# A SwiGLU down projection in split fp32r, with the FFN width worked in two halves

## The reference, cut to what matters

```python
h = h + mix
xn = rmsnorm(h, norm_ffn)
gate, up = split_cols(xn @ ffn_w_gu, (FFN_HIDDEN, FFN_HIDDEN))     # 1024 x 5632
h = h + (jax.nn.silu(gate) * up) @ ffn_w_down                      # 2816 x 1024
y = rmsnorm(h, norm_final)
```

## Time and profile before

| what | value |
| --- | --- |
| median of 3 runs | 3121.63 us |
| the profiled execution: its span, first to last instruction | 3120.6 us |
| gate and up, first matmul to the first of down | 2283.98 to 2784.48 us of the span |
| down, to the start of the last norm's sums | 2784.48 to 3089.9 us |
| last norm and stores | 3089.9 to 3120.6 us |
| mean granted TensorE clock | 0.933 |

### The profile page before, as it was taken

One profiled execution on the slowest core, in us unless ns is written; L12 is line 12 of the kernel. 1 busy time (PEld: TensorE's weight loads), 2 busy tenths in 40 slices (PEclk: granted clock), 3 DMA queues, 4 the chain that ended last, 5 costly groups with the idle time before them and its releaser, 6 DMA issues.

```text
span 3120.6 us, 46699 instructions
## 1 busy us (share of the span) xinstructions
PE 2861.2 (92%) x19365; PEld 2259.2 (72%) x19365; DVE 975.0 (31%) x1690; ACT 706.4 (23%) x1113; POOL 19.1 (1%) x26
## 2 busy tenths in 40 slices
PE   5979797989999999999999999964979999999997
PEld 3657575757777686868677786853979999986665
DVE  1120302035354453636354443636131111110001
ACT  2221202122232322222232322221132222210000
POOL 0000000000000000000000000000000000000000
PEclk8989797979998999999998999956989999999999
DMA  3010101000000000000000000002001111120111
GB/s 132 14 70 0 69 0 69 28 15 1 29 2 29 2 29 2 19 11 2 29 2 29 2 29 2 28 15 108 27 27 47 47 47 47 45 78 19 37 37 54
DMA packets 19098, 99.84 MB, mean 32 GB/s; under 512 B 4544, under 2 KB 4736, under 8 KB 15120
## 3 DMA queue, kind: packets, MB, share of 16 engines
q1 hardware_dynamic: 17328, 88.44, 7.7%
q0 software_dynamic: 1632, 9.21, 0.8%
HBM read 86.31 MB, written 11.34 MB: 31 GB/s over the span
## 4 chain that ended last, share of the span: by engine, by line
PE 89%; DVE 6%; issue 2%; ACT 2%; DMA 0%; DVEq 0%; SPq 0%; ACTq 0%
PE bank L502 89%; ACT arena L870 1%; DMA arena<-in_consts 0%; DVE arena L1418 0%; DVE arena L1269 0%; DVE arena L1417 0%; DVE arena L1271 0%; DVE arena L1429 0%; DVE arena L1182 0%; DVE arena L1570 0%; ACT L870 0%; DVE arena L1256 0%; DVE merged_low L1500 0%; DVE arena L1589 0%; DVE x_low L1574 0%
## 5 line engine op out<-in xcount | busy, mean ns | idle before, releaser
L502 PE MATMUL bank<-arena 64*64 64x64 f32 (+7 forms) x15586 | 2263.9, 320 | 214.5 <-DVE arena L1528 58.0
L502 PEld LDWEIGHTS bank<-arena 128*128 128x128 f32 (+1 forms) x15586 | 1662.3, 174 | 814.3 <-issue 387.8
L502 PE MATMUL bank<-merged_high,gate_up_high 128*128 128x344 f32 x1056 | 338.7, 321 | 23.5 <-DVE gate_up_low L1559 23.5
L502 PE MATMUL bank<-x_low,gate_up_high 128*128 128x344 f32 x1056 | 338.0, 320 | 0.0
L502 PE MATMUL bank<-merged_high,gate_up_low 128*128 128x344 f32 x1056 | 337.9, 320 | 0.0
L870 ACT ACTIVATE arena<-arena 128x64 f32<-128x64 f32 (+7 forms) x289 | 178.2, 634 | 658.8 <-DVE arena L1585 309.5
L502 PEld LDWEIGHTS bank<-merged_high,gate_up_high 128*128 128x128 f32 x1056 | 199.0, 188 | 24.0 <-issue 24.0
L1045 ACT COPY arena<-arena 64x512 f32<-64x512 f32 x192 | 118.2, 616 | 413.6 <-DVE arena L1461 398.1
L502 PEld LDWEIGHTS bank<-merged_high,gate_up_low 128*128 128x128 f32 x1056 | 199.1, 189 | 0.0
L502 PEld LDWEIGHTS bank<-x_low,gate_up_high 128*128 128x128 f32 x1056 | 199.0, 188 | 0.0
L870 ACT ACTIVATE arena<-bank,arena 128x348 f32<-128x348 f32 (+3 forms) x180 | 97.0, 547 | 320.1 <-PE bank L502 311.1
(11 more groups left out here) (134 smaller groups left out, 1109.0 us busy)
## 6 DMA issues: line engine op xcount, KB each, us to landing
arena<-in_w_gu SPq DMA_DIRECT2D x44, 512.0 KB, 3.6
arena<-in_w_pair SPq DMA_DIRECT2D x8, 2112.0 KB, 8.0
arena<-in_w_gla SPq DMA_DIRECT2D x4, 3072.0 KB, 9.5
arena<-in_w_d SPq DMA_DIRECT2D x7, 1408.0 KB, 6.0
arena<-in_xT SPq DMA_DIRECT2D x16, 516.0 KB, 7.2
out_yT<-arena SPq DMA_DIRECT2D x8, 516.0 KB, 3.0
arena<-in_gla_s POOLq DMA_DIRECT2D x4, 1024.0 KB, 5.1
out_glas<-arena POOLq DMA_DIRECT2D x4, 1024.0 KB, 4.1
```

Of the source, the lines that this page charges most:

```text
L502: return nc.tensor.matmul(out, lhsT, rhs, start=start, stop=stop)
```

## The change

The FFN width is worked in two halves of 11 tiles (KH). Each half g runs gate and up for its 11 tiles and then down over these 11 tiles for all 8 output tiles, and VectorE adds each half's result to H. Down uses the split: the products silu(gate) x up are rounded to `ACHR` by ScalarE (`products_high`), and VectorE leaves the rest in place as `ACLR` (`products_low`). Down's weights come in two units of 6 and 5 width tiles for each m, through the same two buffer sets as the gate and up weights, and are split in the same way (`weights_high`, `weights_low`).

```diff
+KH = FT // 2
+UNITS = [(0, 6), (6, 5)]
+        ACHR = rounded("act_high", A0, KH * TS)
+        ACLR = rounded("act_low", A0 + KH * TS, KH * TS)
+        ACTV = rounded("act", A0 + KH * TS, KH * TS, F32).rearrange("p (k t) -> p k t", t=TS)
...
+        J_HALF = 2 * KH + KT
+        J_N3 = J_FFN + 2 * J_HALF + 1
+        WEIGHTS = 2 * KH + 2 * KT
...
+            for g in range(2):                                        # SyncE
+                j0 = J_FFN + g * J_HALF
+                if g == 1:
+                    for q in range(2):
+                        if q == 0:
+                            sp.wait_ge(down_used, KT)
+                        else:
+                            sp.wait_ge(done[2], j0)
+                        sp.dma_start(WGL[q]..., w_gu[KH, :, q * D:(q + 1) * D]).then_inc(gu_loaded[q], 16)
+                with sp.Fori(1, KH) as ft:
+                    for q in range(2):
+                        sp.wait_ge(done[2], ft * 2 + (j0 - 1 + q))
+                        sp.dma_start(WGL[q]..., w_gu[ft + g * KH, ...]).then_inc(gu_loaded[q], 16)
+                for m in range(KT):
+                    for u, (k0, n) in enumerate(UNITS):
+                        if m == 0:
+                            sp.wait_ge(done[2], j0 + 2 * KH - 1 + u)
+                        elif u == 0:
+                            sp.wait_ge(down_used, g * KT + m)
+                        else:
+                            sp.wait_ge(done[2], j0 + 2 * KH + m)
+                        sp.dma_start(WGL[u]...[:, 0:n * P], w_d[m, :, c0:c0 + n * P]).then_inc(gu_loaded[u], 16)
...
-            def down(m, odd, loads):                                  # TensorE
-                gate(wd_loaded[odd], loads)
-                for b, (c0, n) in enumerate(TB):
-                    gate(out_of[b], m + J_DOWN)
-                    for kt in range(FT):
-                        last = mm(bank[b][:, 0:n], WD[odd][:, kt, :], ACTV[:, kt, c0:c0 + n], kt == 0, kt == FT - 1)
-                    last.then_inc(done[b], 1)
+            def down(g, m):
+                j0 = J_FFN + g * J_HALF + 2 * KH
+                for u, (k0, count) in enumerate(UNITS):
+                    gate(gu_lo, m * 2 + (g * WEIGHTS + 2 * KH + u + 1))
+                    gate(act_lo, g * KH + k0 + count)
+                    for b, (c0, n) in enumerate(TB):
+                        if u == 0:
+                            gate(out_of[b], m + j0)
+                        for k in range(count):
+                            mm(bank[b][:, 0:n], hi, xh, u + k == 0, False)
+                            mm(bank[b][:, 0:n], hi, xl, False, False)
+                            last = mm(bank[b][:, 0:n], lo, xh, False, u == 1 and k == count - 1)
+                        if u == 1:
+                            last.then_inc(done[b], 1)
+                    if u == 0:
+                        last.then_inc(down_used, 1)
+            for g in range(2):
+                with pe.Fori(0, KH) as ft:
+                    ...                                               # gate and up as before
+                with pe.Fori(0, KT) as m:
+                    down(g, m)
...
+                with act.Fori(1, KH) as ft:                           # ScalarE, in each half
+                    weights_high(0, D, ft * 16 + (l0 + 16))
+                    weights_high(1, D, ft * 16 + (l0 + 16))
+                    products_high(ft - 1, g)
+                    silu(ft, j0)
+                weights_high(0, UNITS[0][1] * P, ...)
+                products_high(KH - 1, g)
+                weights_high(1, UNITS[1][1] * P, ...)
+                with act.Fori(1, KT) as m:
+                    for u in range(2):
+                        weights_high(u, UNITS[u][1] * P, ...)
+                if g == 0:
+                    weights_high(0, D, HALF_LOADS + 16)
...
+                weights_low(w0 + 2 * KH - 1, 1, D)                    # VectorE, end of each half
+                products_low(KH - 2, g)
+                up(KH - 1, g, j0)
+                w0 = w0 + 2 * KH
+                weights_low(w0, 0, UNITS[0][1] * P)
+                products_low(KH - 1, g)
+                weights_low(w0 + 1, 1, UNITS[1][1] * P)
+                with dve.Fori(0, KT - 1) as m:
+                    weights_low(m * 2 + (w0 + 2), 0, UNITS[0][1] * P)
+                    down_out(m)                                       # adds the 3 banks to H[:, m, :]
+                    weights_low(m * 2 + (w0 + 3), 1, UNITS[1][1] * P)
+                if g == 0:
+                    weights_low(WEIGHTS, 0, D)
+                down_out(KT - 1)
```

More of the change, by code:

```diff
@@ L92, in hybrid_step, with rounded @@
     with ExitStack() as ctx:
-        def rounded(name, off, n):
+        def rounded(name, off, n, kind=F32R):
             with ExitStack() as below:
@@ L97, in rounded @@
                     below.enter_context(nc.sbuf_tensor(name + "_below", [P, off], F32))
-                return below.enter_context(nc.sbuf_tensor(name, [P, n], F32R))
+                return below.enter_context(nc.sbuf_tensor(name, [P, n], kind))
         A0 = 24832 + NCONST + 3 * KT
@@ L266, in hybrid_step @@
         assert C_BONES + 4096 <= C_EPS and C_ONES + 128 <= C_BONES
[L267 to L272, removed]
+        assert A0 + FT * TS <= 53200, A0
         Y_SQ = [at(TS * kt, TS) for kt in range(KT)]
@@ L366, in hybrid_step @@
         gu_hi, gu_lo = sem("gate_up_high_ready"), sem("gate_up_low_ready")
-        wd0_loaded = [sem(f"first_down_loaded{j}") for j in range(2)]
-        wd_loaded = [sem(f"down_loaded{j}") for j in range(2)]
+        down_used = sem("down_first_unit_used")
+        prod_ready = sem("gate_times_up_ready")
+        act_hi, act_lo = sem("act_high_ready"), sem("act_low_ready")
         yn_ready = sem("y_ready")
@@ L378, in hybrid_step @@
         J_FFN = J_N2
-        J_DOWN = J_FFN + 2 * FT
-        J_N3 = J_DOWN + KT + 1
+        J_HALF = 2 * KH + KT
+        J_N3 = J_FFN + 2 * J_HALF + 1
+        WEIGHTS = 2 * KH + 2 * KT
         SLOTS = 3 * NC
@@ L450, in _ @@
                                  ).then_inc(wo_loaded[j], 16)
[L451 to L464, removed]
+            for g in range(2):
[6 more added lines that the diff above has]
+                            sp.wait_ge(done[2], j0)
+                        sp.dma_start(WGL[q].rearrange("p k n -> p (k n)"), w_gu[KH, :, q * D:(q + 1) * D]
+                                     ).then_inc(gu_loaded[q], 16)
+                with sp.Fori(1, KH) as ft:
+                    for q in range(2):
+                        sp.wait_ge(done[2], ft * 2 + (j0 - 1 + q))
+                        sp.dma_start(WGL[q].rearrange("p k n -> p (k n)"), w_gu[ft + g * KH, :, q * D:(q + 1) * D]
+                                     ).then_inc(gu_loaded[q], 16)
+                for m in range(KT):
[6 more added lines that the diff above has]
+                            sp.wait_ge(done[2], j0 + 2 * KH + m)
+                        c0 = (g * KH + k0) * P
+                        sp.dma_start(WGL[u].rearrange("p k n -> p (k n)")[:, 0:n * P], w_d[m, :, c0:c0 + n * P]
+                                     ).then_inc(gu_loaded[u], 16)
             for kt in range(KT):
@@ L833, in _ @@
             pe.wait_ge(x_lo, KT)
-            with pe.Fori(0, FT) as ft:
-                for q in range(2):
-                    gate(gu_lo, ft * 2 + (q + 1))
-                    for b, (c0, n) in enumerate(TB):
[L838 to L842, removed]
-                for b, (c0, n) in enumerate(TB):
[L844 to L849, removed]
-                        last.then_inc(done[b], 1)
@@ L852, in down @@
-            def down(m, odd, loads):
-                gate(wd_loaded[odd], loads)
-                for b, (c0, n) in enumerate(TB):
-                    gate(out_of[b], m + J_DOWN)
-                    for kt in range(FT):
-                        last = mm(bank[b][:, 0:n], WD[odd][:, kt, :], ACTV[:, kt, c0:c0 + n], kt == 0, kt == FT - 1)
[L858 to L862, removed]
@@ L863, in _ @@
-            down(KT - 1, 1, 16 * (KT // 2))
+            def down(g, m):
[3 more added lines that the diff above has]
+                    gate(act_lo, g * KH + k0 + count)
+                    for b, (c0, n) in enumerate(TB):
+                        if u == 0:
+                            gate(out_of[b], m + j0)
+                        for k in range(count):
+                            x0 = (k0 + k) * TS + c0
+                            hi, lo = (w[u][:, k * P:k * P + P] for w in (WGHR, WGLR))
+                            xh, xl = (x[:, x0:x0 + n] for x in (ACHR, ACLR))
+                            mm(bank[b][:, 0:n], hi, xh, u + k == 0, False)
[5 more added lines that the diff above has]
+                        last.then_inc(down_used, 1)
@@ new lines, in _ @@
+            for g in range(2):
+                j0 = J_FFN + g * J_HALF
+                with pe.Fori(0, KH) as ft:
+                    for q in range(2):
```

(76 more changed lines are left out.)

## The result

The changed kernel takes 3069.57 us (median of 4 runs, 3067.6 to 3071.96) against 3121.53 us: a ratio of 0.9837, 95% interval 0.9823 to 0.9851. The forecast was 3071.5 us. Its profiled execution, the slowest of the four (3071.96 us), has a span of 3070.4 us, 50.2 us less than that of before.

A forecast was written before the change was run, and what follows sets the result against it. TensorE, busy for 92% of the span, was taken as the bound. A 56.1 us gain in down's matmuls, less 4.2 us of waits and 1.8 us of clock, gave 50.1 us and 3071.5 us, range 3066 to 3080, reaching to 3086.

The forecast's parts named there:

- The main term: Down: 1584 fp32r matmuls at gate and up's 0.1574 us take 249.3 us instead of 305.4, a gain of 56.1 us.
- The wait ahead of each half's down: Where each half's down begins, TensorE waits 2.1 us for `up` and the weights' subtraction on VectorE; twice, 4.2 us.
- The clock behind it: After the wait ahead of down, granted clock falls for one of two gaps: 1.8 us lost, bounds 0 and 3.6.
- three rows behind the guess: Profiled gaps of 2.76 and 2.36 us were followed by about 0.5 granted clock, one of 1.78 us by 1.00.
- The weights inside down: Down's unit 0 reload, cast and subtraction take 5.6 of 7.1 us cover; hidden, 1.5 us to spare.
- The first rival: Weights bind partly in down: TensorE waits some 2 us for each of 14 tiles, 27 us, 3099 us; chance 0.09.
- The slower rival: Weights bind outright in down: landings of 10.1 us, 87 us of waiting, 3158 us; chance 0.03.
- Between the halves: Second half's first gate block loads behind down's last unit 0, just hidden; nothing taken, 0.7 us as bound.
- the changes of loop and the other added work: Three added loop changes might cost 8 us (3080 us); added casts, subtractions, additions and loads in down stay hidden.
- A float32 call against three products: In down, one float32 call takes 0.578 us, 3.7 fp32r matmuls, so three products in its place are less work.
- The Trainium skill's rule: Halved array rate makes a float32 call two passes; down would go from 166 to 249 us, 83 us more.
- The sum: Whole kernel: 56.1 - 4.2 - 1.8 = 50.1 us gained; span 3070.5 us, plus 1.0 us for the median, 3071.5 us.

The follow-up runs named there:

- the run with the wait taken away: Changed kernel with the first unit's `weights_low` moved ahead of `up` on VectorE, run twice: 3067.3 and 3066.26 us, ratios 0.9828 and 0.9825.

## Why the prediction was right, point by point

- **The main term**, 1584 matmuls at gate and up's 0.1574 us for 249.3 us, was measured at 125.10 us for each half (2537.69 to 2662.79, 2914.50 to 3039.60): 250.2 us, 0.158 each. The gain of it was 55.2 us where 56.1 stood. That the price is one of the product, and that the halves give nothing, is shown by the runs with four products and with float32 halves.
- **The wait ahead of each half's down** was 2.35 and 2.38 us where 2.1 stood, 4.7 in place of 4.2 us. The place and the cause are shown by taking it away. What was short: 0.14 us between `up` and the subtraction on VectorE, and 0.45 in place of 0.34 us from there to TensorE.
- **The clock behind it**, 1.8 us for one of two gaps, was nothing in the first profile of the changed kernel and 3.2 us for two falls in the second. The price of a fall was about right; how many there are in an execution was a guess. Of four profiled executions with both gaps of 2.35 us (the changed kernel twice, two and four products) three had no fall and one had two. One of the three rows behind the guess was misread, too: ahead of the one of 1.78 us the clock was already at its low level, so that row shows a clock that rose and not one that was kept:

```profile
2083.00:2086.80 3.80, 3.80 (x8) 1.85 (x6) 1.03 (x2) 2.67 (x13) 0.80 (x2) 0.54 0.05 13
```

- **The weights inside down** were hidden, as forecast: in the first half's last tile the subtraction for unit 0 ends at 2645.28, and TensorE needs it at 2537.69 + 7 x 15.64 = 2647.2. The margin was read as 1.5 us up to the subtraction; with the addition behind it, which released TensorE in the run with two products, it is 1.3. The first rival (27 us) needed landings of 6.0 us; they took 3.1. The slower rival has the same place: the run with units of 8 and 3 shows that it can bind without a late DMA, since 2.8 us less cover and a larger unit brought the time back to 3119 us.
- **Between the halves** there was no wait, as taken. That the changes of loop and the other added work cost nothing is shown by the run with the wait taken away, where TensorE's 4800 matmuls are one piece.
- **A float32 call against three products.** The Trainium skill's rule in Perfetto Trace Analysis, section Engine Utilization, as the prediction applied it to a whole call, isn't borne out: with three products the kernel gains 52 us, with four it loses 33. A call leaves two records of 0.289 us, 1.8 fp32r matmuls each, so applied to each record the same factor would come close. The Trainium skill's page FP8 and Floating Point Precision, section TensorE Precision Notes, counts four passes for true float32. The rows are nearer to that than to two, since a call's 0.578 us is 3.7 fp32r matmuls of 0.158 us; no row shows single passes. An fp32r matmul costs a little more than a quarter of a call, which is why four of them cost more than one call.
- **The sum**: 55.2 - 4.7 = 50.5 us inside the two profiles, and 50.2 of the span, since the FFN began 0.3 us later; 50.1 was forecast. The right answer rests on terms whose mechanism was right. That their errors (0.9 and 0.5 us against the gain, 1.8 for it) leave 0.4 us is in part luck, since in the second profile the clock cost 3.2 us. The 1.0 us added from span to median was no fixed distance either: the changed kernel's runs lie 1.5 to 1.6 us above their own spans, so that the profiled one took 3071.96 us; the median of the four is 1.9 us under the forecast.

## What to carry to other kernels

A split into three fp32r products pays against a float32 matmul by the price of the products alone, here 0.474 against 0.578 us for 344 columns; a product more undoes it, and so does cover too short for the split weights' chain of load, rounding, subtraction and release. Look up that chain in a stage that already runs it, set it against the matmuls that run meanwhile, and cut the units so that the smaller one still covers the larger one's reload. And at each change of stage ask what stands ahead of the first step on each engine: a subtraction whose data had long been there waited behind work that could only end with TensorE, and moving it one place up took 4.6 us out of the stretch.

## What was not expected of the hardware

Behind waits of TensorE of one length, in a stream otherwise dense, the granted clock was kept in some places and fell in others. Behind the two of 2.2 us ahead of down it was 1.00 in one profile of the changed kernel, and also in the runs with two and with four products; in the other profile of the changed kernel it was 0.5 to 0.6 behind both. With units of 8 and 3 it fell behind 11 of 17 waits of 2.0 to 2.5 us, and those behind which it was kept are neither the shortest nor the longest. Behind waits of 0.8 to 1.1 us (two products) the 66 matmuls of a tile took 10.6 to 10.7 us throughout, so it didn't fall, and behind two of 4.4 us it fell both times. A fall cost 1.4 to 1.6 us, once 2.6. What decides between the two within one length isn't shown; that it is where the wait lies in time, as was supposed before the changed kernel was run again, stays untested.
